# Nine 1024-wide norms: their sums of squares accumulated chunk by chunk by TensorE instead of added up by VectorE

## What is computed

```
def rms_norm(x, g):                      # first block: attn_norm and ffn_norm of 2 layers, final_norm
    y = xf * lax.rsqrt(jnp.mean(xf * xf, axis=-1, keepdims=True) + EPS)
    return y * g

def _layer_norm(x, g, b):                # second block: ln1 and ln2 of 2 layers
    mu = jnp.mean(xf, axis=-1, keepdims=True)
    var = jnp.mean(jnp.square(xf - mu), axis=-1, keepdims=True)
    return (xf - mu) * lax.rsqrt(var + LN_EPS) * g + b
```

## Time and profile before

| | |
|---|---|
| median of 3 runs | 3326.69 us |
| the profiled execution | 3324.52 us |
| its span in the trace | 3322.9 us |
| TensorE busy | 3126.1 us (94%), 14074 records |
| VectorE busy | 1675.2 us (50%), 3077 records |
| ScalarE busy | 847.0 us (25%) |
| GpSimd busy | 1370.4 us (41%) |
| mean granted clock of TensorE | 0.955 of full |

### The profile page before, as it was taken

The page is one execution under the profiler, slowest core; times in us unless marked ns, Lnnn a source line. Parts: engine busy times, 40 slices in busy tenths (PEclk is TensorE's granted clock), DMA queues, the critical chain, the costliest instruction groups (busy, mean ns, idle before and its releaser), DMA issues.

```text
span 3322.9 us, 40340 instructions
## 1 busy us (share of the span) xinstructions
PE 3126.1 (94%) x14074; PEld 2449.6 (74%) x14074; DVE 1675.2 (50%) x3077; ACT 847.0 (25%) x1855; POOL 1370.4 (41%) x924
## 2 busy tenths in 40 slices
PE   6999999999989999989999979999799999899997
PEld 5756778877656778878666768888686666688885
DVE  4575475463675557454851653333438516533334
ACT  2346221121355212121333321111123333200112
POOL 4210455555210555554223435555342234355552
PEclk9988999999979999999999989999899999899998
DMA  6210455555210555555223436655452234455652
GB/s 245 96 57 24 156 182 192 194 197 190 101 37 26 194 179 194 193 200 165 89 89 114 155 124 196 203 193 194 146 165 89 89 114 153 141 188 195 203 196 89
DMA packets 136517, 493.99 MB, mean 149 GB/s; under 512 B 15280, under 2 KB 15536, under 8 KB 136112
## 3 DMA queue, kind: packets, MB, share of 16 engines
q0 software_dynamic: 66240, 241.20, 22.7%
q1 hardware_dynamic: 68544, 245.40, 21.6%
q10 hardware_dynamic: 1584, 5.33, 0.5%
HBM read 489.77 MB, written 2.10 MB: 148 GB/s over the span
## 4 chain that ended last, share of the span: by engine, by line
PE 81%; DVE 12%; ACT 3%; issue 2%; DMA 1%; POOL 0%; SPq 0%; DVEq 0%; POOLq 0%
PE ps L467 22%; PE ps L469 20%; PE ps L468 20%; PE ps L620 6%; PE ps L643 5%; DVE cv L1199 2%; PE ps L633 2%; DVE tmp L1207 2%; DVE cv L1201 1%; PE ps L576 1%; PE ps L577 1%; PE ps L578 1%; DVE rx L914 1%; PE ps L530 1%; PE ps L539 1%
## 5 line engine op out<-in xcount | busy, mean ns | idle before, releaser
L467 PE MATMUL ps<-hi,w_hi 128*128 128x512 f32 x3216 | 1291.2, 402 | 51.5 <-DVE lo L890 18.5
L468 PE MATMUL ps<-hi,w_lo 128*128 128x512 f32 x3216 | 1266.2, 394 | 0.0
L469 PE MATMUL ps<-lo,w_hi 128*128 128x512 f32 x3216 | 1265.8, 394 | 0.0
L443 POOL TENSOR_TENSOR w_lo<-w_raw,w_hi 128x1024 fp32r<-128x1024 f32 x460 | 1111.9, 2417 | 69.7 <-DMA w_hi<-weights 59.2
L438 POOL DMA_DIRECT2D w_hi<-weights x460 | 261.6, 569 | 1835.5 <-PE ps L469 1704.4
L467 PEld LDWEIGHTS ps<-hi,w_hi 128*128 128x128 f32 x3216 | 611.4, 190 | 246.6 <-issue 87.7
L469 PEld LDWEIGHTS ps<-lo,w_hi 128*128 128x128 f32 x3216 | 611.5, 190 | 131.1
L468 PEld LDWEIGHTS ps<-hi,w_lo 128*128 128x128 f32 x3216 | 612.1, 190 | 121.0
L974 DVE CUSTOM_DVE_ANT_0 pr<-ps,kc 128x128 f32<-128x128 f32 (+1 forms) x208 | 88.9, 427 | 332.1 <-PE ps L620 330.9
L890 DVE TENSOR_TENSOR lo<-tmp,hi 128x512 fp32r<-128x512 f32 x130 | 184.4, 1418 | 87.0 <-ACT hi L1381 86.7
L1455 ACT ACTIVATE pT<-ps 128x128 f32<-128x128 f32 (+1 forms) x248 | 97.8, 394 | 356.8 <-PE ps L633 356.7
(11 more groups left out here) (265 smaller groups left out, 3237.0 us busy)
## 6 DMA issues: line engine op xcount, KB each, us to landing
w_raw<-weights SPq DMA_DIRECT2D x460, 512.0 KB, 3.4
w_hi<-weights POOLq DMA_DIRECT2D x460, 512.0 KB, 3.8
x<-xt SPq DMA_DIRECT2D x8, 256.0 KB, 16.8
out<-x SPq DMA_DIRECT2D x8, 256.0 KB, 2.0
kc<-k ACTq DMA_DIRECT2D x1, 1216.0 KB, 5.1
bias<-relb ACTq DMA_DIRECT2D x2, 512.0 KB, 15.9
bias<-relb ACTq DMA_DIRECT2D x1, 1024.0 KB, 4.8
praw<-pt ACTq DMA_DIRECT2D x2, 512.0 KB, 3.5
```

Source lines behind the costliest of these rows:

```text
L443: nc.gpsimd.tensor_tensor(wlo[s][:, :], raw[s][:, :], whi[s][:, :].bitcast(F32), ALU.subtract).then_inc(w_split, 1)
L467: nc.tensor.matmul(out_ap, w[0], xx[0], start=first, stop=False)
L468: nc.tensor.matmul(out_ap, w[1], xx[0], start=False, stop=False)
L469: return nc.tensor.matmul(out_ap, w[0], xx[1], start=False, stop=last)
```

## The change

`add_square` is no longer called for the nine norms. A new `square_sums` on TensorE waits for each square (`sq_ready`), runs the four ones-matmuls on its `sq` buffer, and accumulates in the same four PSUM columns over the eight chunks; after each chunk it releases the buffer itself. VectorE's `factors` waits for the eighth release. `sums` stays for the means, and for one 384-wide norm of each layer of the first block. The stream of ScalarE is the same.

```
+            def square_sums():
+
+                for c in range(NC_):
+                    pe.wait_ge(sq_ready, q.sq + c + 1)
+                    for tb in range(NTB):
+                        last = nc.tensor.matmul(ps[:, 4 + tb, 0:1], sq[(q.sq + c) % 4][:, tb * P:(tb + 1) * P], ones,
+                                                start=(c == 0), stop=(c == NC_ - 1))
+                    last.then_inc(sq_used, 1)
+                q.sq += NC_
+
             def input_norm():
                 if q.bca:
                     pe.wait_ge(r_ready, q.bca)
-                q.sq += NC_
-                pe.wait_ge(sq_used, q.sq)
-                sums()
+                square_sums()
...
-                q.sq += NC_
-                pe.wait_ge(sq_used, q.sq)
-                sums()
+                square_sums()
...
-                for c in range(NC_):
-                    add_square(c)
+                q.sq += NC_
...
-                factors([(0, 1, D)], 1, EPS, 0)
+                factors([(0, 1, D)], 1, EPS, NC_)
...
                 for c in range(NC_):
                     V.tensor_tensor(x[:, c, :], x[:, c, :], ps[:, 3, :], ALU.add).then_inc(x_ready, 1)
                     q.x += 1
-                    if c:
-                        add_square(c - 1)
-                add_square(NC_ - 1)
-                factors([(0, 1, D)], 1, LN_EPS, 0)
+                q.sq += NC_
+                factors([(0, 1, D)], 1, LN_EPS, NC_)
```

More of the change, by code:

```diff
@@ L930, in prep @@
                     q.chunk += 1
-                for c in range(NC_):
-                    add_square(c)
+                q.sq += NC_
             def factors(ranges, n_cols, eps, n_chunks, times=None):
                 if n_chunks:
-                    q.sq += n_chunks
                     dve.wait_ge(sq_used, q.sq)
```

## The result

| | before | after |
|---|---|---|
| median, runs | 3323.41 us, 4 runs (3313.49 to 3327.83) | 3376.11 us, 4 runs (3367.49 to 3385.66) |
| profiled execution | 3324.52 us | 3373.32 us |
| TensorE busy, records | 3126.1 us, 14074 | 3224.3 us, 14578 |
| VectorE busy, records | 1675.2 us, 3077 | 1611.4 us, 3014 |
| mean granted clock | 0.955 | 0.948 |

The ratio is 1.0166 (95% interval 1.0133 to 1.0199), so the change makes the kernel slower by 55 us (44 to 66) by the ratio; the two medians lie 52.7 us apart. The forecast was 3375 us, +51 us against the profiled execution of before, which was 48.8 us faster than that of after.

The account below looks back on a forecast made before the run. TensorE was taken as the bound (81% of the chain). Feed-forward +24.2, attention +6.4 and +4.4, final +0.2 and layer norms +15.7 sum to +50.9 us on 3324.52: 3375 us, range 3350 to 3393.

Parts of the forecast that it names:

- TensorE is the path, VectorE's additions are worth only their waits: All nine norms: removing 50 us of VectorE additions can win only TensorE's waits for them, together 54 us.
- The new stream: 64 records, 0.90 us a chunk at full clock, 1.73 at low: Each changed norm's TensorE sums: 64 records instead of 8; eight records take 0.90 us at full clock, 1.73 at low.
- One-column matmuls treat the clock as idleness does: In each norm's new matmuls: clock falls about 3.6 us after the last dense matmul, and never rises again within the stream.
- After the stream the low stretch goes on, 5.1 us: Dense matmuls following the sums stay at the low clock for 5.1 us on average, losing 2.4 us.
- First attention norm, +6.4: First attention norm: sums end 5.9 us later, and the low stretch adds 0.5; 6.4 us slower.
- Final norm, +0.2: Final norm: the new sums end at 1493.2 instead of 1493.06; 0.2 us slower.
- Layer norms +15.7: Four layer norms: sums run at the low clock throughout, 13.8 us; 3.9 us slower each, 15.7 together.
- Rival 1: All nine norms: the new stream keeps or brings the clock to full; sum -8 us, 3316 us; chance 9%.
- Rival 2: Feed-forward part: TensorE's delay vanishes in slack because VectorE is nearly as busy; +26.7 us, 3351 us; chance 5%.
- Rival 3: New sums: accumulating chunks serialises, each record lasting 0.35 us; about +80 us on top, 3455 us; chance 3%.
- rival 4: The change doesn't do what it says, for instance chunks hide while dense tiles still wait; 3325 us; chance 3%.
- The estimate by the load time of the Trainium skill: New matmuls: 107 ns per 128-column load, 0.85 us a chunk at either clock, total about +4 us; the prediction rejected it.

Follow-up runs that it names:

- the wide form: The changed kernel with 128 columns of ones streamed through each new matmul instead of one, timed against the kernel before: 3327.08 us, ratio 1.0011.
- its parts: Three kernels with the change at some norms only, against the kernel before: feed-forward 3345.99 us, layer norms 3341.15 us, attention and final norms 3338.35 us.

## Why the prediction was right

- *TensorE is the path, VectorE's additions are worth only their waits.* Right: the additions lost 50.0 us of busy time, as forecast (all of VectorE lost 63.8), and the kernel became slower.
- *The new stream: 64 records, 0.90 us a chunk at full clock, 1.73 at low.* Right. The layer norm's 64 records take 13.81 us, that is 1.73 a chunk; in the feed-forward norm the stream begins with 11 records to the microsecond.
- *One-column matmuls treat the clock as idleness does.* Right, and by the wide form shown and not only argued. This was read from groups of 24 records inside attention. The fall comes 3.1 us after the start of the stream at the first feed-forward norm; 3.6 had been assumed. The traces have ten such streams of 64 records that begin at the full clock (five of the changed kernel, five of its parts); in all ten it falls, 2.4 to 5.4 us in. The advice of the Trainium skill (TensorE: Matmul & The Clock Gate, "Why this matters for your kernels") to keep TensorE continuously busy is not enough by this: here TensorE is busy all along, and its clock falls.
- *After the stream the low stretch goes on, 5.1 us.* Right in kind; 6.1 us at the first feed-forward norm. This is most of the difference between +12.1 and +12.7.
- *First attention norm, +6.4.* The size was off, +4.6: the stream took 10.2 us (40.41 - 30.20) and not 11.35, since I let the clock fall 2.7 us in, as after the idle time of before, and it fell 3.6 us in. In the kernel with the attention and final norms alone the same norm cost 6.2, with the fall 3.1 us in. The moment of the fall varies from one execution to the next, and this term with it.
- *Final norm, +0.2.* -0.6: an old wait of 8.3 us exchanged for a stream as long, as forecast.
- *Layer norms +15.7.* +15.1 in the trace, and +16 (11 to 22) in the kernel that has only these.
- *Rival 1* did not occur with one column; with 128 columns it does, at +4 and not at -8. Its terms for the feed-forward and attention norms held, those for the final and the layer norms did not: 3.4 us at the low clock still follow the spread.
- *Rival 2*, absorption, is excluded by the kernel with the feed-forward norms alone. Its premise was a misreading: in the feed-forward nets of before TensorE is 98% busy and VectorE 61% (222.5 of 363 us from 402 to 765), so VectorE had slack there and the delay was still not absorbed. That fits the argument against the rival, that VectorE's start shifts with the factor.
- *Rival 3*, serial accumulation, is excluded by the pitch, and *rival 4* by the timeline: the stream begins where the last matmul of the second tile ends.
- *The estimate by the load time of the Trainium skill* (same page, "LDWEIGHTS (loading the stationary operand)"), 107 ns for 128 columns, is not what these runs show at 1.2 GHz. There it is 216 ns a record; at 2.4 GHz it is 110. The prediction put the 216 down to float32 paying twice. That was wrong: float32r has the same 216, so it goes with the clock. What float32 pays twice is the number of records, which the sum had counted, so the total did not suffer.
- Two slips did not enter the sum. "In place of 75" in the upper bound should be 63, as the sentence goes on to say. And a later fall of the clock saves 0.9 us for each us, not 0.8 (one more us at the full clock makes 1.1 chunks, of 1.73 us each at the low one).

Luck had a part in how close the total is. In the trace the terms of the attention norms were too high by 2.2 us and those of the feed-forward norms too low by 1.2. The falls of the clock scatter by 3 us from stream to stream, so a single trace could have lain several us off.

## What to carry to other kernels

Moving work off a half-idle engine gains only the waits that it causes; price what takes its place on the bounding engine at each place apart, above all where the old work was hidden. A matmul with one column and 128 loaded ones cost here as much as one with 128 columns streamed, and twice that in float32. A stream of them lets TensorE's clock fall even with no gap; streaming 128 columns for one kept it up here at no price. Where the sum of a few buffers is wanted, let the idle engine add them if that is hidden; otherwise give them to TensorE in float32r, if rounded summands will do.

## What the runs showed of the hardware that was not expected

- 128 columns instead of one in each of 288 matmuls made the kernel about 50 us faster (3376.11 to 3327.08, each against its own runs of before: 1.0166 and 1.0011), because the granted clock stayed at 1.00 in the feed-forward norms and came up within the layer norms.
- A float32r matmul leaves one record of the kind of which float32 leaves two, at the same pitch: 0.216 us at the low clock (32 in 6.99 us), 0.109 at the full one (32 in 3.49 us).
- VectorE's instructions with two inputs are long where they meet GpSimd's subtraction (L443). Of the L890 instructions of before, 63 take over 2 us, and every one of them overlaps a subtraction by 1.5 us or more; the other 74 take 0.69 us and overlap by 0.44 at most. One of the old additions of squares is of this kind (3.26 us from 765.78, GpSimd from 766.13); it makes most of the 3.6 us wait at the second attention norm of before. In the traces of the two kernels that change only the feed-forward norms no addition meets a subtraction there, TensorE does not wait at that norm, its clock does not fall, and the norm takes 7.1 us less, though nothing in it was changed.
- Runs of one kernel spread by 8 to 25 us here, and in the traces the unchanged attention of a layer differs by up to 7 us between before and the kernel with the attention and final norms. Meetings of the kind just named are one source of it; what share they have was not measured. Effects under 5 us can be read at their place in the trace, but not in the total.
